# Rows that begin at multiples of 64 bytes for the gated and the merged activations of a hybrid decoder layer

## The reference: what is computed

```python
h = einsum('bsd,de->bse', x, w_in)          # q, k, v (3 groups x 8 heads), z_attn, u_pool, z_pool, gates
# branch A: for each head three causal dilated windows; their outputs mixed by softmax denominators
y_attn = o * silu(z_attn)                    # (256, 1024)
# branch B: trailing mean over 2, 4, 8 or 16 tokens minus the token, a 256x256 map per group
y_pool = causal_pool_mixer(u_pool, w_pool, pool_scale) * silu(z_pool)      # (256, 1024)
gates = sigmoid(g_pre + b_gate)
merged = g_attn * (y_attn @ w_proj_attn) + g_pool * (y_pool @ w_proj_pool)  # (256, 2048)
out = merged @ w_out
return layer_norm(DEEPNORM_ALPHA * x + out, ln_gamma, ln_beta)
```

## Time and profile before

| | us |
|---|---|
| median of 3 runs | 953.0 (952.9 to 953.33) |
| the profiled execution | 952.73 |
| its span, first to last instruction | 951.0 |
| TensorE busy in it | 940.2 (99%) |
| VectorE busy | 638.2 (67%) |
| ScalarE busy | 422.9 (44%) |

### The profile page before, as it was taken

How to read it: one execution, slowest core, us unless ns; L and a number is a source line. 1 busy time by engine, 2 the same in 40 slices (tenths; PEclk the granted TensorE clock), 3 DMA queues, 4 the chain that set the end, 5 groups by cost and what they waited for, 6 DMA issues and landing times.

```text
span 951.0 us, 15052 instructions
## 1 busy us (share of the span) xinstructions
PE 940.2 (99%) x5388; PEld 836.1 (88%) x5388; DVE 638.2 (67%) x1004; ACT 422.9 (44%) x594; POOL 0.2 (0%) x4
## 2 busy tenths in 40 slices
PE   8999999999999999999999999999999999999996
PEld 7898998998998998998998999888888888888886
DVE  6767567567567567567567568666666666566866
ACT  6454354354354354354354355544445444443340
POOL 0000000000000000000000000000000000000000
PEclk9999999999999999999999999999999999999999
DMA  9645544544544544545544546555455554557432
GB/s 366 243 175 177 182 173 177 181 172 176 183 170 176 188 164 176 191 162 179 193 157 178 198 155 237 211 184 207 176 180 196 182 192 176 190 200 274 177 133 89
DMA packets 26680, 178.30 MB, mean 187 GB/s; under 512 B 3359, under 2 KB 3615, under 8 KB 6047
## 3 DMA queue, kind: packets, MB, share of 16 engines
q1 hardware_dynamic: 26208, 173.79, 50.0%
q10 hardware_dynamic: 452, 4.24, 1.1%
HBM read 175.92 MB, written 2.10 MB: 187 GB/s over the span
## 4 chain that ended last, share of the span: by engine, by line
PE 97%; DVE 1%; DMA 1%; ACT 0%; SPq 0%; issue 0%; DVEq 0%
PE proj_ps L334 40%; PE proj_ps L335 20%; PE attn_ps L334 6%; PE attn_ps L328 4%; PE attn_ps L330 4%; PE attn_ps L329 4%; PE attn_ps L335 3%; PE value_ps L328 3%; PE value_ps L330 3%; PE value_ps L329 3%; PE mixed_ps L328 1%; PE mixed_ps L330 1%; PE mixed_ps L329 1%; PE mixed_ps L449 1%; DMA first_raw<-in_first 1%; PE attn_ps L410 1%
## 5 line engine op out<-in xcount | busy, mean ns | idle before, releaser
L334 PE MATMUL proj_ps<-xt,w_hi 128*128 128x512 f32 x1648 | 578.2, 396 | 1.8 <-DVE w_lo L750 1.6
L335 PE MATMUL proj_ps<-xt,w_lo 128*128 128x256 f32 x1648 | 459.2, 279 | 0.0
L725 DVE TENSOR_TENSOR w_lo<-w_raw,w_hi 128x1024 fp32r<-128x1024 f32 x314 | 369.2, 1220 | 72.0 <-ACT w_hi L576 70.7
L334 PEld LDWEIGHTS proj_ps<-xt,w_hi 128*128 128x128 f32 x1648 | 309.7, 188 | 75.5 <-issue 1.8
L576 ACT ACTIVATE w_hi<-w_raw 128x1024 fp32r<-128x1024 f32 x314 | 314.1, 1051 | 43.4 <-PE mixed_ps L330 26.4
L335 PEld LDWEIGHTS proj_ps<-xt,w_lo 128*128 128x128 f32 x1648 | 310.6, 188 | 0.1
L596 ACT ACTIVATE corr<-proj_ps 128x256 f32<-128x256 f32 x103 | 39.6, 384 | 290.8 <-PE proj_ps L335 290.8
L739 DVE TENSOR_TENSOR qk_f<-proj_ps,corr 128x256 f32<-128x256 f32 x47 | 19.9, 424 | 77.7 <-ACT corr L596 77.7
L334 PE MATMUL attn_ps<-ya,w_hi 128*128 128x512 f32 x128 | 45.3, 394 | 0.0
L334 PE MATMUL attn_ps<-yp,w_hi 128*128 128x512 f32 x128 | 45.1, 392 | 0.0
L329 PE MATMUL attn_ps<-w_lo,xt 128*128 128x384 f32 x128 | 42.9, 335 | 0.0
(11 more groups left out here) (168 smaller groups left out, 929.2 us busy)
## 6 DMA issues: line engine op xcount, KB each, us to landing
w_raw<-in_weights SPq DMA_DIRECT2D x158, 1024.0 KB, 4.8
first_raw<-in_first SPq DMA_DIRECT2D x6, 640.0 KB, 9.3
res<-in_x_rows ACTq DMA_DIRECT2D x1, 2048.0 KB
out_rows<-res SPq DMA_DIRECT2D x8, 256.0 KB, 2.1
first_raw<-in_first SPq DMA_DIRECT2D x4, 320.0 KB, 4.0
gamma<-in_gamma_row ACTq DMA_DIRECT2D x1, 1024.0 KB
beta<-in_beta_row ACTq DMA_DIRECT2D x1, 1024.0 KB
mask<-in_mask SPq DMA_DIRECT2D x1, 576.0 KB, 16.8
```

The lines of the kernel that those rows point to most:

```text
L334: mm(bank, w_hi[:, slot, cols], tile.rearrange("p a s -> p (a s)"), start=first, stop=False)
L335: return mm(bank[:, SEQ:2 * SEQ], w_lo[:, slot, cols], tile[:, 0, :], start=False, stop=last)
L725: tt(w_lo[:, slot, cols], w_raw[:, slot, cols], w_hi[:, slot, cols].bitcast(F32), ALU.subtract).then_inc(lo_split, 1)
```

## The change

The start of `ya` is rounded up from 124704 to 124736. The tiles behind it begin 32 bytes further on, so that they move by 64 in all. `yp` and `merged` move by 96. A start divided by 64 leaves, before and after:

| tile | before | after |
|---|---|---|
| `ya` | 124704, rest 32 | 124736, rest 0 |
| `p_hi`, `p_lo`, `szp`, `corr`, gates, `q_hi` ... `inv`, `res` | rest 32 | 64 further, rest 32 |
| `yp` | 175904, rest 32 | 176000, rest 0 |
| `merged` | 192288, rest 32 | 192384, rest 0 |
| `first_raw`, `zeros`, `gamma`, `rows` (placed from `ya`), `yp_f` (placed from the end of `merged`) | rest 32 | rest 0 |
| `xt`, `w_raw`, `w_hi`, `w_lo`, the small tiles | unchanged | unchanged |

On each engine the instructions, their order and their waits stay as they were; only addresses differ.

```diff
+LINE = 64
+
@@
-        at_ya = at
+        at_ya = (at + LINE - 1) // LINE * LINE
         at, (ya,) = place(at_ya, [("ya", [HEADS, 2, SEQ], F32R)])
-        at_p = at
+        at_p = at + LINE // 2
         at, (p_hi, p_lo) = place(at_p, [("p_hi", [POOL_TILES, SEQ], F32R),
                                         ("p_lo", [POOL_TILES, SEQ], F32R)])
@@
         _, (zeros,) = place(at_ya, [("zeros", [512], F32R)])
 
-        end_b, (yp, merged) = place(at_phase, [
+        end_b, (yp, merged) = place(at_phase + LINE // 2, [
             ("yp", [POOL_TILES, 2, SEQ], F32R), ("merged", [OT, 2, SEQ], F32R)])
```

## The result

The changed kernel is slower: 957.1 us against 953.0, and the ratio of all runs is 1.0052 with a 95% interval of 1.0041 to 1.0064 (five runs of each; two of the changed kernel's took 959.3, which puts the ratio above that of the medians). Forecast was 949.2, with a range up to 954.8.

What follows compares the result with a forecast made beforehand. TensorE's matmul pace was taken to bound the kernel; 952.7 for the profiled execution − 3.1 (stage B) − 0.7 (stage C) = 948.9, or 949.2 us against the 953.0 median. The range of 8 in 10 was 948.3 to 954.8.

Steps and rivals of the forecast that it cites:

- What bounds the kernel: Whole kernel: TensorE busy 940.2 of 951.0 us, so apart from both ends only the pace of matmuls can change the time.
- two paces on the same tile: `xt` chunks in stages A and B: 0.347 or 0.353 us per k-tile, read as a held rhythm, reset by stalls or remainder changes.
- Everything else moves by exactly 64 and keeps its remainder. By the rows this costs nothing: Remaining moved tiles, stage A's included: same remainder modulo 64, so no cost.
- rival 3: Shifted other tiles throw stage A's loop into the slow rhythm: +6.3 us, 959; chance 0.08 together with the unforeseen.
- after each of its stalls: Argument against a slow stage A: its loop comes out at 5.55 us a chunk after stalls, in all seven passes.
- Stage B, −3.1: Stage B: all 48 chunks at 5.55 us, 266.4 instead of 269.53, as the fast starting rhythm passes through the y chunks.
- rival 2: Stage B's y chunks join the slow pace: +1.5 us, up to 955.8 with stage C worse; chance 0.20.
- keep whatever rhythm stands: Stage B: rest-0 moving rows hold the pace they were set in, fast or slow.
- always come out at 5.55: Stage B's y chunks: moving rows at rest 32 take 5.55 us a chunk, the fast pace.
- Stage C, −0.7, bounds −1.3 and +1.3: Stage C, `merged` at rest 0: L328 loses its excess of 5 to 7 ns in 112 triples, −0.7 us.
- Writes, loads, order, 0: ScalarE and VectorE writes, loads into `first_raw`, unchanged matmul order: cost 0; loads bounded at 0.1 us either way.
- The rules: Two skill pages weighed: by 16-byte lines the change is worth nothing, 953.0; by free stationary loading `merged`'s −0.7 would be 0.

Runs made afterwards that it cites:

- e9: Kernel before, with only `pt` and the stage A tiles behind it moved by 128 bytes: 957.9 us, ratio 1.0054.
- e10: Kernel before, with only `pt` and the stage A tiles behind it moved by 256 bytes: 952.8 us, ratio 1.0001.
- e11: Changed kernel, with the tiles behind `ya` moved by 256 in all; `ya`, `yp`, `merged` keep its remainders modulo 256: 951.9 us, ratio 0.9992.
- f2: e7 with `ya` at remainder 96 modulo 256 and all stage A tiles moved by 256: 948.7 us, ratio 0.9960.
- e5: Kernel before, with `xt` moved by 32 bytes and everything behind it by 128: 951.8 us, ratio 0.9988.
- e7: Kernel before, with `yp` moved by 64 bytes and `merged` by 96; `ya` and all of stage A stay: 948.0 us, ratio 0.9955.
- e2: Kernel before, with only `merged` moved, by 32 bytes: 951.1 us, ratio 0.9982.
- e12: Kernel before, no address moved, one more matmul of 128 columns behind each y chunk: 954.5 us, ratio 1.0017.
- e1: Kernel before, with only the tiles behind `ya` moved by 64 bytes, `yp` and `merged` included: 955.7 us, ratio 1.0029.
- e4: Kernel before, with `yp` moved by 32 bytes and `merged` by 64; stage A's tiles and `ya` stay: 952.9 us, ratio 1.0000.

## Why the prediction was wrong

- *What bounds the kernel*, and that only the pace of matmuls can change: right. So was the reading of two paces on the same tile as a rhythm that is set by what came before. e9 shows it where the tiles being read have not moved. One row was misplaced: the earlier trace rows are of the first head, which ends at 79.8 us, and not of the loop. The loop has the same 5.55 (the chunks from 85.42 to 107.61), so the number stands; but the first head has both paces and not only the slow one.
- *"Everything else moves by exactly 64 and keeps its remainder. By the rows this costs nothing"*: this step failed, and it decided the sign. A move by 64 is not neutral, only one by 256 was (e10, e11), so that these tiles did not keep what matters: `pt` from 32 to 96 costs 4.4 us, `s_sb` 1.1. It was rival 3, to which I had given 0.08 with the unforeseen. I priced it well (6.3 for 63 chunks; 51 chunks became slow, 5.6 with the stretches around them), but argued it away with the loop's coming out at 5.55 "after each of its stalls". That row was measured with `pt` and `s_sb` at 32: it says that stalls do not harm, not that the places do not matter.
- *Stage B, −3.1*: measured +1.2. The y chunks went to 5.62, which is rival 2 (+1.5), and the xt chunks stayed slow. Rows at a multiple of 64 do not "keep whatever rhythm stands"; in the first y chunk of the changed kernel the fast rhythm that came in was lost. Nor do rows at rest 32 "always come out at 5.55": at 96 modulo 256 they took 5.64 (f2). That a fast stage B was there to be had was right (266.2 in e5, 267.3 in e7), but not with aligned rows.
- *Stage C, −0.7, bounds −1.3 and +1.3*: the direction was right, the term mis-sized and its bounds too narrow: −2.2. I let only L328 fall, to its neighbours; in fact all three fell below the fastest row I had, to 389 ns or 227 from start to start.
- *Writes, loads, order, 0*: right as far as can be seen: the three chunks abreast end anywhere between 24.4 and 25.6 us in the profiles of all these kernels.
- *The rules.* By the Trainium skill, "SBUF — State Buffer", section "Door 1: The DMA port swizzle", SBUF is read in lines of 16 bytes. All moves here are multiples of 16, so by that rule none of them could matter. The runs differ: `pt` by 128 bytes cost 5.1 us, by 256 nothing. By the Trainium skill, "TensorE: Matmul & The Clock Gate", section "Part 2: What happens when you issue a matmul", loading stationary blocks takes no read bandwidth from the running matmul. Here `merged`, which TensorE only ever holds, moved by 32 bytes in e2 and the triples went from 0.700 to 0.687 us, while a load of its blocks takes 188 ns in both traces. So what the prediction drew from that sentence, that `merged`'s place cannot matter, does not hold. The measurements decide; whether it is read bandwidth that is lost, or what else in the reading, no run here shows.

Open stays why 256, why just these places, and what sets the rhythm where the places are the same: e12 was the only try at the rhythm itself, and its extra matmul did not change it.

## What to carry to other kernels

When a kernel is bound by back-to-back matmuls, a moved buffer can change the pace of the matmuls behind it, its own readers or not: move one tile at a time by amounts that leave the others at the same remainder modulo 256. Compare the pace of stretches that do not touch what was moved. Aligning more strictly is not by itself better. With the weights at 128, rows at 32 streamed best of the places tried for `ya` and `yp`, while 32 was among the worst for the stationary `merged`; a stationary operand was best at the remainder that the moving one has. Read such gains stage by stage, since a rhythm can differ by 0.1 us a chunk between executions with the same places, as in the first head.

## What the runs showed of the hardware that I had not expected

- The pace of a k-tile (512 and 256 columns) takes a few fixed values, 0.347 and 0.353 us above all, repeated to 0.01 us per chunk over hundreds of microseconds and over different kernels (e1 and the changed kernel, stage A's loop).
- Triples of 512 columns by the place of `merged`, with the weights at 128: 0.681 at 128, 0.687 at 64, 0.697 at 0, 0.700 at 32 and 96 (e1, e4). In e5, with `merged` at 160 and the weights at 0, also 0.700.
- Moving `ya` and `yp`, with the weights at 128: a chunk takes 5.55 to 5.56 at 32 and 32, 5.59 at 32 and 64, 5.60 at 32 and 96, 5.62 at 64 and 128, 5.63 at 64 and 0, 5.64 at 64 and 96 or at 96 and 96.
- The same addresses and instructions can run at either pace: three q and k chunks of the first head take 5.75, 5.65 and 5.66 in the profile of the kernel before and 5.66, 5.55 and 5.55 in that of e12.
